# Query and key tiles stored in high and low parts by the projection, and four smaller moves, in a one-core attention and FFN block

## The reference

```python
def reference(x, c, positions, ada_w, ada_b, norm_attn_g, w_in, ...):
    mod = silu(c) @ ada_w + ada_b
    sh1, sc1, g1, sh2, sc2, g2 = jnp.split(mod, 6, axis=-1)
    h = modulate(rms_norm(x, norm_attn_g), sh1, sc1)
    x = x + g1[:, None, :] * hybrid_mixer(h, positions, w_in, b_forget, dsa_norm_g, fox_norm_g, w_out, 256)
    h = modulate(rms_norm(x, norm_ffn_g), sh2, sc2)
    x = x + g2[:, None, :] * swiglu(h, w_gate, w_up, w_down)
    return rms_norm(x, final_norm_g)

def hybrid_mixer(h, positions, w_in, b_forget, dsa_norm_g, fox_norm_g, w_out, k_top):
    proj = h @ w_in        # q, k, v of 8 DSA heads; indexer; q, k, v of 8 FoX heads; forget gates
    q_d, k_d = rope_partial(q_d), rope_partial(k_d)     # the first 16 of each head's 64 entries
    o_d = dsa_attention(...)     # per query the 256 keys with the highest indexer score, causal
    o_f = fox_attention(...)     # causal, logits + cum(log_f)[q] - cum(log_f)[k]
    y = jnp.concatenate([rms_norm(o_d, dsa_norm_g), rms_norm(o_f, fox_norm_g)], axis=-1)
    return y @ w_out
```

## Time and profile before

| | us |
|---|---|
| median of three runs | 1389.47 |
| lowest and highest run | 1384.02, 1390.10 |
| the profiled execution | 1383.56 |
| its span in the trace | 1381.8 |
| PE busy | 1309.9 |
| DVE busy | 1004.5 |
| POOL busy | 851.4 |
| ACT busy | 695.7 |

### The profile page before, as it was taken

The page is one execution under the profiler, slowest core; times in us unless marked ns, Lnnn a source line. Parts: engine busy times, 40 slices in busy tenths (PEclk is TensorE's granted clock), DMA queues, the critical chain, the costliest instruction groups (busy, mean ns, idle before and its releaser), DMA issues.

```text
span 1381.8 us, 19486 instructions
## 1 busy us (share of the span) xinstructions
PE 1309.9 (95%) x6595; PEld 1069.4 (77%) x6595; DVE 1004.5 (73%) x1585; ACT 695.7 (50%) x1395; POOL 851.4 (62%) x552
## 2 busy tenths in 40 slices
PE   1999999999989999999999899999999999999996
PEld 0988778888767677678887688888888888788885
DVE  4563769999786888876569776655556667479998
ACT  6623345564478777774336344333444333554545
POOL 0261403324359744951027889988889984798995
PEclk9799999999999999999999999999999999999998
DMA  9131312342345776715100333233333234998873
GB/s 382 55 98 55 97 49 92 107 124 78 100 124 168 232 218 192 215 48 198 42 36 31 105 107 123 85 115 100 115 114 109 90 122 153 390 355 300 287 255 140
DMA packets 130379, 200.53 MB, mean 145 GB/s; under 512 B 10637, under 2 KB 65093, under 8 KB 129258
## 3 DMA queue, kind: packets, MB, share of 16 engines
q1 hardware_dynamic: 130282, 199.30, 43.2%
HBM read 156.99 MB, written 42.27 MB: 144 GB/s over the span
## 4 chain that ended last, share of the span: by engine, by line
PE 77%; DVE 10%; issue 4%; ACT 3%; DMA 2%; POOL 2%; SPq 1%; DVEq 0%; ACTq 0%; POOLq 0%
PE PS L2176 20%; PE PS L2177 20%; PE PS L2178 20%; PE PS L2393 4%; PE PS L2345 4%; DVE AS L2042 2%; PE PS L2364 2%; DMA ada<-in_ada_w_dram 1%; DVE BS L2047 1%; POOL WSf L1025 1%; PE PS L2369 1%; PE PS L2366 1%; DVE LP L1815 1%; POOL WS L1037 1%; DVE PS L2099 1%
## 5 line engine op out<-in xcount | busy, mean ns | idle before, releaser
L1037 POOL TENSOR_TENSOR WS<-WSf,WS 128x512 fp32r<-128x512 f32 x109 | 161.7, 1491 | 9.1 <-ACT WS L1347 9.1
L1347 ACT CAST WS<-WSf 128x512 fp32r<-128x512 f32 x110 | 68.5, 623 | 195.3 <-POOL WSf L1025 194.5
L1025 POOL TENSOR_TENSOR WSf<-rawg 128x512 f32<-128x512 f32 x55 | 77.7, 1412 | 115.5 <-PE PS L2178 110.8
L2176 PE MATMUL PS<-yh,WS 128*128 128x512 f32 (+2 forms) x360 | 139.2, 387 | 1.5 <-DVE yl L1956 1.5
L2177 PE MATMUL PS<-yl,WS 128*128 128x512 f32 (+2 forms) x360 | 138.9, 386 | 0.0
L2178 PE MATMUL PS<-yh,WS 128*128 128x512 f32 (+2 forms) x360 | 138.8, 385 | 0.0
L2176 PE MATMUL PS<-BS,AS 128*128 128x512 f32 x308 | 121.0, 393 | 3.9 <-DVE BS L2047 3.1
L2177 PE MATMUL PS<-BS,AS 128*128 128x512 f32 x308 | 120.4, 391 | 0.0
L2178 PE MATMUL PS<-BS,AS 128*128 128x512 f32 x308 | 120.3, 391 | 0.0
L1268 ACT ACTIVATE LP<-LP,nmin 128x128 f32<-128x128 f32 (+7 forms) x128 | 100.2, 783 | 36.5 <-DVE nmin L1815 35.1
L2042 DVE TENSOR_TENSOR AS<-rawa,AS 128x512 fp32r<-128x512 f32 x77 | 100.1, 1316 | 23.5 <-ACT AS L1406 23.3
(11 more groups left out here) (340 smaller groups left out, 3836.0 us busy)
## 6 DMA issues: line engine op xcount, KB each, us to landing
rawb<-in_w_down_dram SPq DMA_DIRECT2D x132, 256.0 KB, 4.8
rawa<-gu_scratch SPq DMA_DIRECT2D x77, 256.0 KB, 4.8
gu_scratch<-GS SPq DMA_DIRECT2D x55, 256.0 KB, 4.8
raw<-in_w_in_dram SPq DMA_DIRECT2D x24, 512.0 KB, 3.9
rawg<-in_w_gate_dram SPq DMA_DIRECT2D x22, 512.0 KB, 4.5
rawu<-in_w_up_dram SPq DMA_DIRECT2D x22, 512.0 KB, 4.4
ada<-in_ada_w_dram SPq DMA_DIRECT2D x8, 1024.0 KB, 15.1
qk_scratch<-stage SPq DMA_DIRECT2D x32, 256.0 KB, 2.2
```

Of the source, the lines that this page charges most:

```text
L1025: pool.tensor_tensor(WSf[m % N_SLOT][:], left(i, mat, a), left(i, mat, b), ALU.add if sign > 0 else ALU.subtract).then_inc(ws_sum, 1)
L1037: pool.tensor_tensor(lo, WSf[m % N_SLOT][:] if b else left(i, mat, a), hi.bitcast(F32), ALU.subtract).then_inc(ws_ready, 1)
L1347: act.copy(WS[m % N_SLOT][:, 0], src).then_inc(ws_hi, 1)
L2176: pe.matmul(dst, left[0], right[0], start=first, stop=False)
```

## The change

1. **Order of the projection.** The chunks are now: indexer, FoX v, FoX q, FoX k, DSA q, k, v. v of FoX came fourth before.
2. **High and low parts are stored.** Each tile of the four q and k chunks is copied twice from PSUM by ACT, into `stage` (float32) and into `stage_h` (fp32r). POOL subtracts (`low_tile`, 128x512) into `stage_l`. SP stores `stage_h` and `stage_l`, to `qk_scratch` and `qk_low_scratch`. POOL's `low_tile` calls stand between the splits of the next chunk's weight pieces.
3. **`prepare` is gone.** `load_qk` loads straight into `QT`, `KA`, `KB` (or `CQ`, `CK`) with six DMAs of 64x1024 for each head in place of four, and waits for PE to have finished the head two before. PE waits for these DMAs (`qk_in`). Head 1 has a QT and KA of its own, where `Qd` and `Kd` were.
4. **`rotate`** runs all at once, in 12 operations of 128x1024 in place of six, since it must join the parts and split them again; it loads and stores four blocks of 512 KB in place of two.
5. **`split_out`** is no longer tied to a head.
6. **DVE's work in attention.** Three tiles of `choice` are done before attention in place of four, and the other five are spread over heads 0 to 4; the modulation operations lie in heads 5 to 11 and 13; three squares move from head 12 to head 10.
7. **`roots(1)`** is at step 12*8+6 in place of 13*8+2.
8. **The FFN start.** ACT rounds block 4 ahead of `root2(7)` and block 5 between `root2(7)` and `scale2(6)`.

The diff, cut to its core:

```diff
-CHUNK_COL = [COL_IDX, COL_FOX, COL_FOX + GW, COL_FOX + 2 * GW, 0, GW, 2 * GW]
+CHUNK_COL = [COL_IDX, COL_FOX + 2 * GW, COL_FOX, COL_FOX + GW, 0, GW, 2 * GW]
-CHOICE_TILES = ((2, 4, 6, 7), (1, 2, 3, 5, 6, 7), (1, 2, 3, 5, 6, 7))
+CHOICE_TILES = ((2, 4, 6, 7), (1, 3, 5, 6, 7), (1, 2, 3, 5, 6, 7), (1, 3, 5, 6, 7), (1, 2, 3, 4))
-MOD_TILES = {hd: (6, 7) if hd < 6 else (1, 2, 6, 7) for hd in (*range(4, 12), 13)}
+MOD_TILES = {hd: (1, 2, 6, 7) for hd in (*range(5, 12), 13)}
+SQUARE_AT = {TT * hd + t: i for i, (hd, t) in enumerate([(10, t) for t in (3, 4, 5)] + [(12, t) for t in range(5)])}
+ROOT_AT = 12 * TT + 6
-WO_HEAD = {0: 12, 1: 12, 4: 13, 5: 13, 6: 14, 7: 14}
-CHOICE_EARLY = 4 * CHOICE_OPS
+CHOICE_EARLY = 3 * CHOICE_OPS
-TURNED = (1, 2, 4, 5)
-VALUES = (3, 6)
+TURNED = (2, 3, 4, 5)
+VALUES = (1, 6)
+LOW_AHEAD = ((0, 1), (2,), (3,), (4,))
...
             def load_qk(hd):
-                if hd >= 1:
-                    sp.wait_ge(k_lo, hd)
-                    sp.wait_ge(q_lo, hd)
-                for i, dst in enumerate((Qd, Kd)):
-                    for half in range(2):
-                        sp.dma_start(dst[half * DH:(half + 1) * DH, :],
-                                     qk_dram[first + i, row:row + DH, :]).then_inc(qk_in[b], 16)
+                if hd >= 2:
+                    sp.wait_ge(qk_pe, TT * (hd - 1))
+                sp.dma_start(QT[i][0:DH, :].bitcast(F32), q_high).then_inc(qk_in[b], 16)
+                sp.dma_start(KA[i][0:DH, :].bitcast(F32), k_high).then_inc(qk_in[b], 16)
+                sp.dma_start(QT[i][DH:P, :].bitcast(F32), q_low).then_inc(qk_in[b], 16)
+                sp.dma_start(KA[i][DH:P, :].bitcast(F32), k_high).then_inc(qk_in[b], 16)
+                if hd < NH:
+                    sp.dma_start(CQ[0:DH, b, :].bitcast(F32), q_high).then_inc(qk_in[b], 16)
+                    sp.dma_start(CK[0:DH, b, :].bitcast(F32), k_low).then_inc(qk_in[b], 16)
+                else:
+                    sp.dma_start(KB[i][0:DH, :].bitcast(F32), k_low).then_inc(qk_in[b], 16)
+                    sp.dma_start(KB[i][DH:P, :].bitcast(F32), k_low).then_inc(qk_in[b], 16)
...
+            def low_tile(ch, t):
+                n = TT * (ch - 1) + t
+                pool.wait_ge(pj_ev, TT * ch + t + 1)
+                pool.tensor_tensor(stage_l[:, n % 2, :], stage[:, n % 2, :], stage_h[:, n % 2, :].bitcast(F32),
+                                   ALU.subtract).then_inc(pj_lo, 1)
             for n in range(N_PROJ):
                 ch = n // PIECES
+                if ch - 1 in TURNED:
+                    for t in LOW_AHEAD[n % PIECES]:
+                        low_tile(ch - 1, t)
...
                 split(n, hi[:, 0:2 * w], lo[:, 0:2 * w], held, rounded=ch == 0).then_inc(w_ready, 1)
+                if ch - 1 in TURNED and n % PIECES == PIECES - 1:
+                    for t in range(LOW_AHEAD[-1][-1] + 1, TT):
+                        low_tile(ch - 1, t)
...
-            for hd in range(2 * NH):
-                if 1 <= hd and hd + 1 < 2 * NH:
-                    prepare(hd + 1)
-                    if hd + 1 in ROPE_HEADS:
-                        rotate(ROPE_HEADS.index(hd + 1))
...
+            pool.wait_ge(tp_ev, group_no["C", 3] + 1)
+            for dst in (g1b, mod23):
+                pool.memset(dst[:], 0.0).then_inc(md_ms, 1)
+            rotate()
+            pool.wait_ge(tp_ev, group_no["M", 5] + 1)
+            pool.memset(mod23[:, 0, :], 0.0).then_inc(md_ms, 1)
+            for k in WO_ORDER:
                 split_out(k)
...
-                    act.wait_ge(stage_out[n % 2], 16 * (n // 2))
-                act.mul(stage[:, n % 2, :], PS[:, q % 4, :], -SOFT if ch in (1, 4) else 1.0).then_inc(pj_ev, 1)
+                    act.wait_ge(stage_out[n % 2], stores_ahead(n))
+                last = act.mul(stage[:, n % 2, :], PS[:, q % 4, :], QK_SCALE.get(ch, 1.0))
+                if ch in TURNED:
+                    last = act.mul(stage_h[:, n % 2, :], PS[:, q % 4, :], QK_SCALE[ch])
+                last.then_inc(pj_ev, 1)
...
-                if s == 13 * TT + 2:
+                if s == ROOT_AT:
                     roots(1)
...
                 if s == TT - 1:
-                    for m in range(4):
+                    for m in range(5):
                         slot_high(m)
                 if s < TT:
                     root2(s)
+                if s == TT - 1:
+                    slot_high(5)
                 if s >= 1:
                     scale2(s - 1)
-            for m in range(4, N_SLOT):
-                slot_high(m)
+            slot_high(6)
...
-                    pe.wait_ge(k_lo, hd + 1)
-                    pe.wait_ge(q_lo, hd + 1)
+                    pe.wait_ge(qk_in[hd % 2], 96 * (hd // 2 + 1))
```

More of the change, by code:

```diff
@@ L203, with stores_through, stores_ahead @@
     GB_TARGET.append((GB_TARGET[_m - DOWN_RAW_B] if _m >= DOWN_RAW_B else GB_BASE[_m]) + (32 if _m in DOWN_SUMS else 16))
-GU_BASE = dict(zip(DOWN, 2 * [8 * (NC - 1) * TT] + [16 * MOD_SLOT.count(0), 16 * MOD_SLOT.count(1)] + 2 * [64 * V_PARTS] + [16]))
+GU_BASE = dict(zip(DOWN, 2 * [8 * TT * (NC - 1 + len(TURNED))] + [16 * MOD_SLOT.count(0), 16 * MOD_SLOT.count(1)] + 2 * [64 * V_PARTS] + [16]))
+def stores_through(ch):
+    return 8 * TT * sum(2 if c in TURNED else 1 for c in range(1, ch + 1))
+def stores_ahead(n):
+    return sum(32 if 1 + m // TT in TURNED else 16 for m in range(n % 2, n, 2))
 def done_first(t):
@@ L686, in _ @@
             for ch in range(1, NC):
-                if ch == 5:
-                    for i in range(2):
-                        sp.wait_ge(stage_out[i], 16 * 3 * TT // 2)
-                    sp.wait_ge(sc_pe, IH * (TT - FIRST_TOPK))
-                    load_qk(0)
                 if ch == 6:
@@ L696, in _ @@
                     load_cum(1)
+                    for i in range(2):
+                        sp.wait_ge(stage_out[i], stores_through(3))
+                    sp.wait_ge(sc_pe, IH * (TT - FIRST_TOPK))
+                    load_qk(0)
                 for t in range(TT):
@@ L700, in _ @@
                     if ch in TURNED:
+                        sp.wait_ge(pj_lo, TT * (ch - TURNED[0]) + t + 1)
+                    if ch in TURNED:
                         f, half = divmod(t, 2)
-                        dst = qk_dram[QK_BASE[ch], f * P:(f + 1) * P, half * BANK:(half + 1) * BANK]
-                    else:
-                        dst = v_dram[VALUES.index(ch), t * P:(t + 1) * P, :]
-                    sp.dma_start(dst, stage[:, q % 2, :]).then_inc(stage_out[q % 2], 16)
+                        for dram, held in ((qk_dram, stage_h), (qk_low_dram, stage_l)):
+                            sp.dma_start(dram[QK_BASE[ch], f * P:(f + 1) * P, half * BANK:(half + 1) * BANK],
+                                         held[:, q % 2, :].bitcast(F32)).then_inc(stage_out[q % 2], 16)
+                    else:
+                        sp.dma_start(v_dram[VALUES.index(ch), t * P:(t + 1) * P, :], stage[:, q % 2, :]
+                                     ).then_inc(stage_out[q % 2], 16)
                     if t < PIECES and ch + 1 < NC:
                         load_piece(PIECES * (ch + 1) + t)
-                    if ch == 6 and t == 4:
+                    if ch == 6 and t == 2:
+                        for i in range(2):
+                            sp.wait_ge(stage_out[i], stores_through(5))
                         load_qk(1)
-                    if ch == 6 and t == TT - 2:
-                        load_qk(2)
                 if ch == 4:
@@ L1876, in _ @@
                     normalise(*NORM_AT[s])
[L1877 to L1878 removed]
+                if s in SQUARE_AT:
+                    square(SQUARE_AT[s], GW, GW, (2, 1))
                 if hd == 14:
```

124 lines of the change are left out of this document (52 added, 72 removed).

## The result

The changed kernel takes 1397.63 us (median of nine runs, 1392.19 to 1399.62). The kernel before took 1386.81 (median of nine, 1384.02 to 1393.79). The ratio is 1.0068, with a 95% interval of 1.0050 to 1.0087: slower by about 9 us, where 10 us faster had been forecast. The profiled execution of the changed kernel has a span of 1397.9 us, against 1381.8.

The account below looks back on a forecast made before the run. PE was taken as the bound, busy 1309.9 of 1381.8 us, with attention's pairs following DVE's work, slowed by POOL. Terms 5 - 14 - 1 = -10 us took the mean 1386.8 to 1377, range 1362 to 1390.

Parts of the forecast that it names:

- part 2: Attention: direct loads in place of `prepare` arrive in time; 0 taken, up to 3 us per head if modulation loads wait.
- Part 1: Attention: without `prepare` on POOL, DVE meets less contention and PE gains; -14 us, range -3 to -24.
- The pair estimates: Attention: changes per pair of heads, -0.5, -2, +2, -2.5, -1.5, 0, -4.5 and -4.5 us, summing to -13.5.
- 29 over 32: Attention: pairs' excess over blocked DVE time, given as 0.84, behind the range's end of -24 us.
- Part 3: Projection: low tiles hold DVE's small bisection operations; +4 us for PE at the last chunk and +1 earlier.
- Part 4: Heads 0 to 4: the moved choice tile's 6.7 us on DVE, counted in the pair estimates.
- Part 5: FFN start: earlier cast of block 4 lets POOL do blocks 4 and 5 earlier; -1 us, -5 to +2.
- D: Rival, chance 0.12: low tiles hold most threshold operations, PE stands 16 to 20 us at the last chunk; 1395 to 1403.
- C: Rival, chance 0.12: ACT's exp and copy chain holds attention's pairs, gain -5, bisection costs 5; 1386 us.
- A: Main case, chance 0.62: the parts as forecast, attention -14 us; 1377 us, with 1370 to 1383.

Follow-up runs that it names:

- three edits: Changed kernel, SP's queue reordered: head 4's gate rows before rotation loads, v stores before head loads, two modulation loads before head 6's q/k; 1380.4 us, ratio 0.9948.
- the kernel with placed low tiles: Kernel with the three edits, POOL's low tiles inside the bisection waiting for DVE's next threshold; 1377.24 us, ratio 0.9905.

## Why the prediction was wrong

**The step that failed is part 2**, the loads. It took 0, with "nothing is late unless SP's queue is held ahead of it by a modulation load", and looked only at whether head 2's loads arrive. The three edits, which touch nothing but SP's order, are worth 16.6 us: with them attention begins with no idle time of PE before it, head 4 starts without a wait, and DVE has no wait for the first modulation's weights. The three faults of that step: it did not ask who stands *behind* the six loads and their new wait (the v stores, the modulation weights); it did not price the rotation's doubled loads by what follows them; and it added durations of issue and landing while the queue's conditions set the times. All three were visible in the order of SP and the table of steps. POOL's wait for Kd, 57.3 us, was read as slack to be gained; the old wait on `k_lo` also let SP pass early to the modulation loads. Before, head 6's q and k loads began at 437.70, 12.4 us into head 4; in the changed kernel they began at 450.03, 17.9 us into it.

**Part 1 was too large.** DVE's operations did get faster about as forecast (the modulations alone from 58.1 to 45.2 us, mean 1.41; 1.35 had been named as the sign). But with the queue mended the heads gave 4.4 us and not 14, and 2.8 of them lie in head 13, from which the root had moved. PE was busy for 238.88 of 253 us, so only 14.1 us were idle at all, and 14 was the whole of it. The pair estimates went by DVE's work and didn't see that some heads are held by PE itself: head 4 of the kernel before took 15.8 us with PE busy throughout, and so did head 6 of the changed one. By pairs the kernel with three edits differs from the kernel before by -1.5, -3.2, +4.9, 0, +0.7, -2.1 and -2.8 us, and by -0.5 in head 14. The forecast was -0.5, -2, +2, -2.5, -1.5, 0, -4.5, and -4.5 for the last pair. About 3 us of the shortfall lie in the pair of heads 4 and 5, beside the rotation, for whose greater length 1 us had been taken; eight of its twelve operations cost that pair 3.8 us, of which head 6 gives 1 back. (In the range, 29 over 32 is 0.91 and not 0.84; nothing else rests on it.)

**Part 3 was right in mechanism and too large at PE.** The bisection ended at 339 where 340 was forecast, but that is partly luck. The low tiles cost it more than nine holds of 1.1 us: with them shrunk to 8 columns it ends 16.4 us earlier, of which 2.2 come from an earlier start. And that end is 8.9 us ahead of the kernel before, so the rest of the new order holds it less than the old one did; why was not tested. At PE +5 had been taken. With the queue mended attention begins at 365.18 for 363.69, which is 1.5 us later, and the idle time at 338 is 1.2 to 1.3 us. The 4.9 us between this kernel and the one with 8 columns is another quantity, of which the traces place 1.5 at the bisection.

**Part 4** was right in giving nothing, as far as the choices go. **Part 5**, with 1 us forecast, and the move of the root, taken as 0, measured 1.1 and 2.2 by the ratios, both within noise.

**The rivals.** D had the right sign, and the measured 1397.63 lies within its 1395 to 1403. That is luck, since its cause is not what happened: it let the bisection end at 350 to 357 and the low tiles hold PE by 16 to 20 us at the last chunk, and in fact the bisection ended at 339 and PE stood there for 1.3 us. C took 5 us for attention's gain, which is nearer to the 4.4 than A's 14. Whether ACT's chain held the pairs, as it said, was not tested: in attention with the three edits PE waits 5.9 us for DVE's maximum and 4.3 for ACT's copies of the transposed tiles.

**How the terms add up.** By the ratios the changed kernel is 0.0068 above the kernel before, and with SP's order mended 0.0052 below it. So the order cost 0.0120 (16.6 us) where 0 was taken, and the rest of the change gives 7 us where 10 was forecast. By the two traces the rest gives only 2.6 (spans 1379.2 and 1381.8): attention begins 1.5 later (+5 forecast), the heads up to the start of head 15 are 4.4 shorter (-14 forecast for all of attention), and what follows is 0.4 longer (-1 forecast). The traces and the medians differ since the profiled execution of the kernel before, 1383.56, is 3.3 us under the median of all its runs. Part of the 7 us can't be placed in the traces, and I leave it open.

## What to carry to other kernels

When a consumer's wait moves from a compute engine into the queue of the engine that issues DMAs, list all that stands behind it in that queue, with the time at which each must be issued; here the order alone, with the same bytes, was worth 16.6 us. Before work is taken off an engine beside the critical one, take the critical engine's own idle time, and what its lowered clock costs, as the upper bound, head by head. A small operation in a serial loop can be held for the whole of POOL's operation beside it, so look at what POOL's work lands on. Moving it beside the counting took that hold away here, and the trace shows 1.4 us of it at PE.

## What was not expected of the hardware

A low tile beside the counting cost nothing, while beside an operation of 128x6 it made 0.17 us into 1.17. First the kernel with placed low tiles, POOL and then DVE, where 0.61 and 0.74 us are the times without a low tile too:

```profile
299.48 1.29 POOL L947 TENSOR_TENSOR stagel<-stage,stageh 128x512 fp32r<-128x512 f32 x1 [2.36 <-DVE bis L1746]
```

```profile
299.37 0.61 DVE L1691 TENSOR_SCALAR_CACHE_REDUCE marks_c<-sel,bis 128x384 f32<-128x384 f32 x1
...
299.90 0.74 DVE L1691 TENSOR_SCALAR_CACHE_REDUCE marks_c<-sel,bis 128x512 f32<-128x512 f32 x1
```

Then POOL's and DVE's rows of the changed kernel:

```profile
300.54 1.29 POOL L934 TENSOR_TENSOR stagel<-stage,stageh 128x512 fp32r<-128x512 f32 x1 [7.03 <-ACT stageh L1164]
```

```profile
300.68 1.17 DVE L1733 TENSOR_TENSOR bis<-bis 128x6 f32<-128x6 f32 x1
```

DVE's operation ends when POOL's does. This agrees with the rule of the Trainium skill named in the prediction ("SBUF — State Buffer", "Who interferes with whom"). The prediction went further than that and called a low tile a hazard wherever it lands; beside the counting, which reads one tile (`sel`), it was none.

A gap of PE can cost more than its length. With a wait of 4.13 us gone, head 4 is 2.6 us shorter as well (17.5 for 20.1), and a gap of 1.23 us in head 13 was followed by 10 us at a granted clock of 0.50. It doesn't always: behind the gap of 1.27 us at 338, and behind one of 1.01 us at 565.83 in the kernel with the three edits, the clock stayed at 1.00.
